# Two stacked decoder blocks in one kernel: c loaded as one row, the last tile pair joined, blocks by seven at odd pairs of chunks

## The reference

```
mod = silu(c) @ w_mod + b_mod                  # c: 2048 values, one row
shift, scale, gate = split(mod, 3)
h = rms_norm(x, g_pre) * (1 + scale) + shift
...
u = max(h2 @ w_up, 0) ** 2                     # 2048 -> 8192
x = x + u @ w_down                             # 8192 -> 2048
```

## Time and profile before

| | us |
|---|---|
| three runs, median (lowest to highest) | 2884.42 (2882.26 to 2884.56) |
| the profiled execution | 2882.08 |
| its span, first to last instruction | 2880.2 |
| PE busy | 2801.0 (97%) |
| DVE busy | 2144.4 (74%) |
| ACT busy | 1511.9 (52%) |
| HBM traffic over the span | 212 GB/s on average, 398 in its first fortieth |

### The profile page before, as it was taken

One profiled execution on the slowest core, in us unless ns is written; L12 is line 12 of the kernel. 1 busy time (PEld: TensorE's weight loads), 2 busy tenths in 40 slices (PEclk: granted clock), 3 DMA queues, 4 the chain that ended last, 5 costly groups with the idle time before them and its releaser, 6 DMA issues.

```text
span 2880.2 us, 37285 instructions
## 1 busy us (share of the span) xinstructions
PE 2801.0 (97%) x14490; PEld 2417.2 (84%) x14490; DVE 2144.4 (74%) x2787; ACT 1511.9 (52%) x2102; POOL 39.4 (1%) x48
## 2 busy tenths in 40 slices
PE   5998998999999999999999999999999999999998
PEld 5887787898889988888888888798888888888887
DVE  8999998689755566667886678745666668866774
ACT  5445554665546554644554455565556445544453
POOL 0000000000000000000000000000000000000000
PEclk9999999999999999999999999999999999999999
DMA  9996597767655454556665566655544556555564
GB/s 398 381 362 227 192 367 299 273 208 259 237 160 179 151 172 150 174 189 194 202 205 184 190 197 199 195 175 155 175 161 161 190 192 202 204 185 189 197 213 153
DMA packets 173887, 611.91 MB, mean 212 GB/s; under 512 B 19680, under 2 KB 19952, under 8 KB 173072
## 3 DMA queue, kind: packets, MB, share of 16 engines
q1 hardware_dynamic: 170912, 600.42, 61.6%
q0 software_dynamic: 1824, 6.61, 0.8%
q10 hardware_dynamic: 976, 2.51, 0.3%
HBM read 607.34 MB, written 2.11 MB: 212 GB/s over the span
## 4 chain that ended last, share of the span: by engine, by line
PE 86%; DVE 9%; ACT 2%; issue 2%; DMA 1%; POOL 0%; SPq 0%; DVEq 0%; POOLq 0%; ACTq 0%
PE ps L2315 16%; PE ps L2246 16%; PE ps L2249 16%; PE ps L2253 16%; PE ps L2325 8%; DVE w_lo L1393 2%; PE ps L2188 2%; DVE raw L1623 2%; PE ps L2289 1%; PE ps L2292 1%; PE ps L2294 1%; PE ps L2525 1%; PE ps L2303 1%; PE ps L2301 1%; PE ps L2298 1%
## 5 line engine op out<-in xcount | busy, mean ns | idle before, releaser
L1393 DVE TENSOR_TENSOR w_lo<-raw,w_hi 128x1024 fp32r<-128x1024 f32 (+3 forms) x942 | 1091.9, 1177 | 522.3 <-ACT w_hi L989 518.5
L989 ACT ACTIVATE w_hi<-raw 128x1024 fp32r<-128x1024 f32 (+3 forms) x942 | 948.7, 1020 | 1006.6 <-PE ps L2253 389.6
L2246 PE MATMUL ps<-w_hi,hT_both 128*128 128x512 f32 (+3 forms) x1824 | 479.1, 384 | 13.0 <-DVE proj L1595 6.7
L2315 PE MATMUL ps<-hT_both,w_hi 128*128 128x512 f32 x2048 | 490.5, 391 | 1.1 <-DVE u L1549 0.9
L2253 PE MATMUL ps<-w_hi,hT_both 128*128 128x512 f32 (+3 forms) x1824 | 458.9, 373 | 0.0
L2315 PEld LDWEIGHTS ps<-hT_both,w_hi 128*128 128x128 f32 x2048 | 376.0, 188 | 75.1 <-DVE u L1549 1.3
L2249 PE MATMUL ps<-w_lo,hT_both 128*128 128x512 f32 (+3 forms) x1640 | 415.3, 375 | 0.6 <-DVE w_lo L1393 0.6
L2253 PEld LDWEIGHTS ps<-w_hi,hT_both 128*128 128x128 f32 x1824 | 338.4, 188 | 48.7
L2246 PEld LDWEIGHTS ps<-w_hi,hT_both 128*128 128x128 f32 x1824 | 327.6, 190 | 59.1 <-DVE proj L1595 10.3
L2249 PEld LDWEIGHTS ps<-w_lo,hT_both 128*128 128x128 f32 x1640 | 305.3, 188 | 45.4 <-DVE w_lo L1393 1.5
L2325 PEld LDWEIGHTS ps<-hT_both,w_lo 128*128 128x128 f32 x2048 | 262.8, 191 | 10.2
(11 more groups left out here) (306 smaller groups left out, 2543.3 us busy)
## 6 DMA issues: line engine op xcount, KB each, us to landing
raw<-in_w_up SPq DMA_DIRECT2D x256, 512.0 KB, 3.8
raw<-in_w_down SPq DMA_DIRECT2D x256, 512.0 KB, 3.6
raw<-in_w_modT SPq DMA_DIRECT2D x162, 512.0 KB, 5.9
raw<-in_w_rest SPq DMA_DIRECT2D x80, 456.0 KB, 3.4
raw<-in_w_z SPq DMA_DIRECT2D x56, 512.0 KB, 4.3
raw<-in_w_out SPq DMA_DIRECT2D x51, 512.0 KB, 4.4
raw<-in_w_oa SPq DMA_DIRECT2D x32, 512.0 KB, 3.4
raw_more<-in_w_modT SPq DMA_DIRECT2D x30, 512.0 KB, 6.1
```

The source lines that it names most:

```text
L989: act.activation(hi_blocks(L % SPLIT_SLOTS, c, w), blocks(raw_at(G), c, w), ACT.Copy).then_inc(S.hi_ready, 1)
L1393: dve.tensor_tensor(blocks(lo_at(G), c, w), blocks(raw_at(G), c, w), hi_blocks(s, c, w).bitcast(F32), ALU.subtract).then_inc(S.group_read, 1)
L2246: pe.matmul(o, rows(hi, c, t), wh[:, c], start=start and c == 0, stop=False)
L2315: pe.matmul(ps[:, bank(job, i, f)], wh[:, c, f * P:(f + 1) * P], hT_both[:, k0 + c].rearrange("p a n -> p (a n)"), start=k0 + c == 0, stop ...
```

## The change

Four edits:

1. `c` is loaded to one partition only (8 KB). PE multiplies a row of ones with it (four float32 matmuls of one row by 512 columns, into four PSUM banks), and ACT applies silu from PSUM in two halves. The waits for the constants count two loads instead of three.
2. In `down11` tiles 2 and 3 are joined too, for groups 0 to 11; groups 12 to 15 of tile 2 and then of tile 3 follow. The second tile pair of `down01` and of `down11` has five blocks by seven (`LAST_QUADS`), all other pairs have six.
3. The buffers of `combine` for `down01` and `down11` lie in the two slots of the ring that are not in use then, and `combos_hi` in the last part of `hT`; the ring goes back to 10 slots one job later in layer 1. The eight turns in which the left side of `c21` is made are spread, -4, -3, -2, -1 in place of -2, -2, -1, -1, and 1 to 4 as before.
4. The blocks by seven stand at j = 1, 3, 5, 7, 9, 11 in place of 2, 4, 6, 8, 10, 12.

```diff
-QUADS = ((2, 4, 6, 8, 10, 12), (2, 4, 6, 8, 10, 12))
+QUADS = ((1, 3, 5, 7, 9, 11), (1, 3, 5, 7, 9, 11))
+LAST_QUADS = (1, 3, 5, 7, 9)
...
+                cut = len(groups) - (self.tail if pair[1] == tiles[-1] else 0)
+                steps += [(i, j) for j in groups[:cut] for i in pair] + [(i, j) for i in pair for j in groups[cut:]]
...
-            Ac = Area(hT_at + 4 * KC * 2 * P) if h else A2s
+            Ac = Area(ring_end - 4 * (RAW_SLOTS - FEW_SLOTS) * GROUP) if h else A2s
...
+            Ac = Area(hT_at + 4 * (2 * KC * 2 * P - 4 * COLS)) if h else A2s
+            combos_hi.append(Ac(f"combos_hi{h}", [P, 3, COLS], F32R))
...
-                            joined=1 if l == DEPTH - 1 and h else 2, quads=QUADS[h]))])]
+                            joined=2, quads=(QUADS[h], LAST_QUADS if h else QUADS[h])))])]
...
-                                                         for kind, h, count in (("c2", "", RAW_SLOTS), ("up", 0, FEW_SLOTS))]]
+                                                         for kind, h, count in (("in2" if l else "c2", "", RAW_SLOTS), ("up", 0, FEW_SLOTS))]]
...
-        lead("c21", *after("c21", -2, -2, -1, -1, 1, 2, 3, 4))
+        lead("c21", *after("c21", -4, -3, -2, -1, 1, 2, 3, 4))
...
-            sp.dma_start(c_row[:].rearrange("p c n -> p (c n)"), io["c"][0].partition_broadcast(P)).then_inc(S.const_landed, 16)
+            sp.dma_start(c_row[0:1].rearrange("p c n -> p (c n)"), io["c"][0:1]).then_inc(S.c_landed, 16)
...
+            pool.memset(ones_row, 1.0).then_inc(S.ones_ready, 1)
...
-            act.wait_ge(S.const_landed, 48)
-            act.activation(c_row[:], c_row[:], ACT.Silu).then_inc(S.c_ready, 1)
+            act.wait_ge(S.c_spread, 1)
+            for h in range(2):
+                act.activation(c_row[:, h], ps[:, 2 * h:2 * h + 2].rearrange("p b n -> p (b n)"), ACT.Silu).then_inc(S.c_ready, 1)
...
+            for k in range(4):
+                mm = pe.matmul(ps[:, k], ones_row, c_row[0:1, k // 2, k % 2 * COLS:(k % 2 + 1) * COLS], start=True, stop=True)
+            mm.then_inc(S.c_spread, 1)
```

More of the change, by code:

```diff
@@ L207, in steps @@
         if self.joined:
-            return ([(2 * p + a, j) for p in range(self.joined) for j in groups for a in range(2)]
-                    + [(i, j) for i in tiles[2 * self.joined:] for j in groups])
+            steps = []
+            for p in range(self.joined):
+                pair = tiles[2 * p:2 * p + 2]
+                cut = len(groups) - (self.tail if pair[1] == tiles[-1] else 0)
+                steps += [(i, j) for j in groups[:cut] for i in pair] + [(i, j) for i in pair for j in groups[cut:]]
+            return steps
         if self.paired:
@@ L219, in seven, with last_seven @@
     def seven(self, i, j):
-        return self.together(i) and j in self.quads
+        return self.together(i) and j in self.quads[i // 2]
+    def last_seven(self, p):
+        return self.steps().index((2 * p + 1, max(self.quads[p])))
     def after_quads(self, i, j):
-        return 2 * (j - max(self.quads) - 1) + i % 2 if self.together(i) else -1
+        return self.steps().index((i, j)) - self.last_seven(i // 2) - 1
     def in_tail(self, i, j):
@@ L407, in build @@
             const_landed = sem("const_landed")
+            c_landed = sem("c_landed")
+            ones_ready = sem("ones_ready")
+            c_spread = sem("c_spread")
             pinned_copied = sem("pinned_copied")
@@ L647, in build @@
         summed = {(job.layer, int(job.name[-1]), j): k
-                  for k, (job, j) in enumerate((job, j) for job in downs for j in job.quads)}
+                  for k, (job, j) in enumerate((job, j) for job in downs for j in job.quads[0])}
         quad_at = {L: k for k, L in enumerate(L for job in downs for q, (i, j) in enumerate(job.steps())
@@ L657, in last_quad @@
         def last_quad(job, p):
-            return quad_at[job.L + job.steps().index((2 * p + 1, max(job.quads)))]
+            return quad_at[job.L + job.last_seven(p)]
         def sums_of(job, i):
             down = jobs["down" + job.name[-2:]]
-            return down.quads.index(i) if i in down.quads else None
+            return down.quads[0].index(i) if i in down.quads[0] else None
         def ahead(jobs_):
@@ L1199, in wide @@
                             squares_of(job, done, junk_m[:])
-                    if i >= 2 and j == 3 and job.name == "down11":
+                    if job.name == "down11" and (i, j) in ((2, 3), (3, 13)):
                         for done in range(2) if i == 2 else (2,):
@@ L1699, in wide @@
                             prev = None
-                        if job.together(i):
+                        if job.together(i) and not (job.tail and i == job.tiles - 1):
                             prev = None
@@ L1706, in wide @@
                         final_columns(j // 7, j // 2 % 2 if j > 5 else j // 4)
-                    if job.name == "down11" and i == 3 and j in (3, 5):
-                        final_columns(i - 1, j // 4)
+                    if job.name == "down11" and (i, j) == (3, 13):
+                        for t in range(TOK):
+                            final_columns(2, t)
                     yield
@@ L2258, in seven_products @@
                 h, q = int(job.name[-1]), quad_at[L]
-                first, last = j == min(job.quads), j == max(job.quads)
+                first, last = j == min(job.quads[p]), j == max(job.quads[p])
                 if first:
@@ L2266, in seven_products @@
                     pe.wait_ge(S.sums_split, summed[job.layer, h, j] + 1)
-                at = job.quads.index(j)
+                at = job.quads[0].index(j)
                 def left(k, t):
```

15 lines of the change are left out of this document (9 added, 6 removed).

## The result

| | before | after |
|---|---|---|
| six runs each, median (us) | 2884.14 | 2901.14 |
| lowest to highest | 2882.19 to 2884.56 | 2897.92 to 2902.58 |
| the profiled execution, its span | 2882.08, 2880.2 | 2899.73, 2897.8 |
| ratio, 95% interval | | 1.0059 [1.0048, 1.0071] |

What follows compares the result with a forecast made beforehand. PE, busy 97% of the span, sets the end by its work and its waits, each ending with one DVE instruction behind others. The terms sum to +18.6 us on 2884.4, giving 2903 us, 80% range 2892 to 2912.

Steps and rivals of the forecast that it cites:

- edit 1, start: Kernel start: 127 fewer copies of 8 KB let the first `w_modT` product start at 11.9; -2.5 us, range -3.2 to 0.
- edit 2, 12 matmuls: Last tile pair: four more blocks by seven save 3 matmuls each, DVE's added work lying beside PE; -2.7 us.
- edit 3, `c21` wait and clock: Start of `c21`: PE waits 1.5 us instead of 3.9, with no clock fall; -4.1 us, range -5.6 to -1.7.
- borders `down` to `up`: Two job borders other than `c21`: PE no longer starts 0.26 us late; -0.5 us.
- edit 4, starts: Four `down` job starts: `square_u` of tile 15 comes later, behind `combine` and the split of sums; +14.6 us.
- edit 4, borders: Tile-pair borders in four `down` jobs: PE waits for tile 1 behind `combine` and a split; +7.0 us, range +2 to +9.
- clock at the starts: Behind the four job-start waits PE falls to half clock, 1.7 us each; +6.8 us, between 3.4 and 10.2.
- The two bounds: Job starts: nothing if DVE's backlog misses `square_u`; 8 us each if ACT's rounding and tile 15 copy come later.
- (a): Rival: DVE gets through in time, no stalls at job starts or borders, only gains stay; 2874.6 us, chance 7%.
- (b): Rival: PE stalls but its clock does not fall; 2896 us, chance 13%.
- (c): Rival: tile-pair borders also fall to low clock, or ACT is last at job starts; 2911 us, chance 15%.
- (d): Rival: the start gains nothing, as the path of `c` ends at 14.4, not 11.9; 2905.5 us, chance 10%.

Runs made afterwards that it cites:

- The order experiments: Changed kernel with tile 15 of `up` squared ahead of splits and `combine` at job starts: 2881.91 us; with tile 1 also taken out earlier at borders: 2876.15 us.
- blocks at even numbers: Changed kernel with edit 4 taken back, edits 1 to 3 kept, blocks by seven at 2, 4, ..., 12 (last pairs to 10): 2875.40 us.
- edit 4 alone: Kernel before the change, with only the blocks by seven moved to 1, 3, ..., 11: 2902.72 us, ratio 1.0068.
- the block at 1: Kernel with edits 1 to 3 and blocks at even numbers, only the first block moved from j = 2 to 1: 2907.11 us, ratio 1.0085.
- the wait on ACT: Changed kernel with the wait for the end of `up` in `down01` and `down11` moved from DVE to ACT: 2894.32 us, ratio 1.0035.
- the old order of `c21`: Kernel with edits 1 to 3 and blocks at even numbers, left-side turns of `c21` back at -2, -2, -1, -1: 2877.97 us.

## Why the prediction was right

| term | predicted | in the changed kernel |
|---|---|---|
| edit 1, start | -2.5 | -1.7 at 91 us; -2.3 at 1343 |
| edit 2, 12 matmuls | -2.7 | -2.7 |
| edit 3, `c21` wait and clock | -4.1 | -4.4 |
| borders `down` to `up` | -0.5 | -0.8 with the `up` jobs |
| edit 4, starts | +14.6 | +13.4 |
| edit 4, borders | +7.0 | +6.3 |
| clock at the starts | +6.8 | +8.2 |
| sum | +18.6 | +17.7 (jobs: +17.57) |

- **What bounds the kernel.** Right: each microsecond of PE's idle time was one of the end, and the ends of the waits were single DVE instructions behind others. The order experiments show it without changing the work.
- **Edit 1.** The direction was right, both numbers were off. The first product starts at 12.58, not 11.9: the missing bytes gave 1.84 us, not 2.5. And the path of `c` was mis-sized: the four float32 products of 512 columns are eight instructions of 0.9 us, 7.19 in all, where I had at most 3.9, since I took the eight instructions of the row for eight products, and each product is two. The term was saved by `c` landing at 2.53 and not at 6.7; `c` was ready at 11.7, just ahead of the load. Since each product is two instructions, PE also has four fewer and not the eight forecast. The rest of the gain depends on the clock in the first block.
- **Edit 2.** The number holds for the changed kernel: `down11` is +5.30, and 4.48 (start) + 1.58 (border) + 2.66 (clock) - 3.40 (15 matmuls) gives 5.32. That DVE's work on the blocks is fully covered doesn't hold with blocks at even numbers: `down11` wins 2.69 over before and not 3.4.
- **Edit 3.** The size was right, the attribution wrong. I took `take_parts` out of the turn in my sum, but counted the gain as one of edit 3; 1.6 of the 2.8 us come from where the last block stands. Its rows also add up to 2.92 + 1.54 = 4.46 us and not 4.65, so to a wait of 1.3 us; 1.06 was measured.
- **Edit 4, starts.** 2.2 and 4.5 in place of 2.6 and 4.7 a start. From the first subtraction to the end of `square_u` DVE took 7.52 us (2360.59 to 2368.11), where I had 7.8 with steps between instructions added; on DVE the next instruction starts a little before the last one's listed end (2360.59, where the split of u is listed to 2360.67). The two bounds (nothing, 8 us each) were not near.
- **Edit 4, borders.** 1.58 each in place of 1.75, and no half clock, as said.
- **Clock.** The number of falls was right, four; two of them lasted twice as long, those after 4.98 us, which the upper bound had named. The Trainium skill ("TensorE: Matmul & The Clock Gate", HAM oscillation — how this bites in real kernels) tells of a kernel in which every wait for a load between two bursts of matmuls made the next burst start at the low clock. The trace agrees for the two waits of 4.98 us, which here are for DVE and not for a load; behind the four of 1.7 us the clock stayed.
- **Rivals.** (a), DVE in time, is out by the waits; (b), no fall, was seen at `down10` with edit 4 alone and with the block at 1, and at `down01` with the wait on ACT, so it is real for single starts and not for all four; (c) happened at one border of another kernel (its 2911 is 2909.8 by its own terms); (d) is out by the first product at 12.58.

That the sum is right within 1.6 us is owed in part to errors that cancel: starts and borders came out 1.9 lower than their terms, the clock 1.4 higher.

## What to carry to other kernels

Before moving a piece of work on an engine with idle time, list what it will stand ahead of: if that is the instruction that frees the buffer of the engine that bounds the kernel, the idle time elsewhere doesn't pay for it, and putting the freeing instruction first costs a few lines. Attribute a gain to the edit that causes it only after taking the edits apart; here two edits won the same microseconds, and the parts summed to 10 us where the whole measured 17. Of a wait, price the clock behind it as a separate term with its own odds.

## What the runs showed of the hardware

- A wait of one length can keep the clock or lose it. Counted from the job `down00` on, in the kernels before and changed, and in those with edit 4 alone, with the wait on ACT, with the block at 1 and with the old order of `c21`: after waits of 4.98 us six of six starts ran on at 0.50; after the one of 3.87, too; after 2.7 us, seven of ten; after 2.25 to 2.47 us, two of six; after the 1.7 us of the borders, none of eleven. Which it is changed for the same place from one kernel to the next: `down10` in the changed kernel 0.50, with edit 4 alone 1.00, both after 2.7 us.
- The lost time is not the same either: where the clock fell, 1.4 to 1.6 us after a wait of 2.7, and 1.6 to 2.9 after one of 4.98.
- The same place can keep the clock in one kernel and lose it in another in the first block too. The wait at 194 us kept it before (2.45 us) and lost it in the changed kernel (2.48 us); the one at 327 us lost it before and kept it in the changed kernel (2.39 us in both).
- A float32 product of one row by 512 columns was two instructions of 0.9 us each at the start of the kernel (7.19 for eight), where the products of rounded values with 512 columns in the `down` jobs take 0.227 one. The profile prints a granted clock of 1.00 for this stretch. Yet eight instructions of 128 columns took 1.94 us at 21.86 and 1.03 at 1852.15, and the profile prints 1.00 for both. Which level the start really ran at stays open.
